# Two tiles' shared down products and the spread of the gates made in the middle of the expert loop

## What is computed

```
t, _ = token_mixer(h)                      # earlier stages
x  = x + gate1 * RMSNorm(t);  h = RMSNorm(x) * (1 + scale2) + shift2
eidx = top-8 of 64 experts per token;  w = gates (sum to 2.5)
routed = sum over the 8 of  w * ((silu(h @ w1[e]) * (h @ w3[e])) @ w2[e])
shared = (silu(h @ ws1) * (h @ ws3)) @ ws2
y = x + gate2 * RMSNorm(routed + shared)
```

## Time and profile before

| | |
|---|---|
| median of 3 runs | 1266.09 us (1265.21 to 1268.41) |
| the profiled execution, its time | 1263.9 us |
| its span, first to last instruction | 1262.2 us |
| PE busy | 1179.9 us, 93% of the span |
| DMA engines, 694 to 1167 us of the span | 90% or more busy, 396 to 414 GB/s |
| expert loop | from about 630 to 1219.5 us of the span |
| tail | from 1219.5 us to the end |

### The profile page before, as it was taken

The page is one execution under the profiler, slowest core; times in us unless marked ns, Lnnn a source line. Parts: engine busy times, 40 slices in busy tenths (PEclk is TensorE's granted clock), DMA queues, the critical chain, the costliest instruction groups (busy, mean ns, idle before and its releaser), DMA issues.

```text
span 1262.2 us, 25654 instructions
## 1 busy us (share of the span) xinstructions
PE 1179.9 (93%) x8947; PEld 849.8 (67%) x8948; DVE 556.5 (44%) x902; ACT 335.0 (27%) x631; POOL 524.5 (42%) x527
## 2 busy tenths in 40 slices
PE   5899999999999899968899999997799998999997
PEld 5599999999999899956655555553445554455442
DVE  0576676659568868136733322211122222222124
ACT  4522322322333442335211211111111111112112
POOL 1244444445448243410655444453345543444410
PEclk8899999999999999989999999998899999999999
DMA  9954245424421233309979999999999999999974
GB/s 300 307 167 151 85 149 165 148 85 150 150 83 34 67 100 100 117 1 382 356 291 393 396 396 409 409 409 414 412 408 409 407 403 401 402 404 404 371 289 168
DMA packets 160169, 337.35 MB, mean 267 GB/s; under 512 B 14686, under 2 KB 99242, under 8 KB 143728
## 3 DMA queue, kind: packets, MB, share of 16 engines
q1 hardware_dynamic: 140048, 295.55, 62.8%
q0 software_dynamic: 16656, 34.14, 7.2%
q10 hardware_dynamic: 3424, 7.09, 1.7%
HBM read 322.21 MB, written 33.30 MB: 282 GB/s over the span
## 4 chain that ended last, share of the span: by engine, by line
PE 71%; DMA 9%; SPq 7%; DVE 5%; issue 5%; POOL 2%; ACT 1%; DVEq 0%; ACTq 0%; POOLq 0%
PE ps L1697 22%; PE ps L1708 11%; PE ps L1459 10%; PE ps L1460 9%; PE ps L1461 9%; DMA w<-in_w_dram 6%; SPq L342 4%; DMA ring<-in_w_ada_dram 2%; SPq L347 2%; PE ps L1703 2%; PE ps L1775 1%; PE ps L1472 1%; PE ps L1414 1%; PE ps L1783 1%; SPq L302 1%
## 5 line engine op out<-in xcount | busy, mean ns | idle before, releaser
L1697 PE MATMUL ps<-w,xe 128*64 x3136 | 369.0, 389 | 35.0 <-DMA w<-in_w_dram 29.3
L1697 PEld LDWEIGHTS ps<-w,xe 128*64 128x64 f32 x3136 | 226.3, 140 | 174.6 <-issue 73.8
L510 POOL TENSOR_TENSOR wsplit<-ring,wsplit 128x1024 fp32r<-128x1024 f32 x80 | 194.6, 2433 | 286.5 <-ACT wsplit L711 276.8
L1459 PE MATMUL ps<-h_s_hi,wsplit 128*128 128x260 f32 x960 | 272.5, 284 | 0.0
L1461 PE MATMUL ps<-h_s_hi,wsplit 128*128 128x260 f32 x960 | 270.9, 282 | 0.0
L1460 PE MATMUL ps<-h_lo_m_hi,wsplit 128*128 128x260 f32 x832 | 235.0, 282 | 0.0
L1337 DVE TENSOR_TENSOR rs<-sg,ps 128x128 f32<-128x128 f32 x98 | 28.2, 288 | 378.7 <-ACT sg L959 378.7
L1708 PE MATMUL ps<-w,eactT 128*64 (+1 forms) x784 | 187.4, 599 | 0.0
L1459 PEld LDWEIGHTS ps<-h_s_hi,wsplit 128*128 128x128 f32 x960 | 180.8, 188 | 6.8 <-issue 5.9
L1461 PEld LDWEIGHTS ps<-h_s_hi,wsplit 128*128 128x128 f32 x960 | 180.9, 188 | 0.0
L711 ACT ACTIVATE wsplit<-ring 128x1024 fp32r<-128x1024 f32 x80 | 84.7, 1060 | 297.9 <-PE ps L1461 287.6
(11 more groups left out here) (323 smaller groups left out, 1346.0 us busy)
## 6 DMA issues: line engine op xcount, KB each, us to landing
w<-in_w_dram SPq DMA_DIRECT2D x192, 1024.0 KB, 19.7
ring<-in_w_in_dram SPq DMA_DIRECT2D x56, 512.0 KB, 4.0
ring<-in_w_ada_dram SPq DMA_DIRECT2D x12, 2048.0 KB, 9.0
act<-y_rows SPq DMA_DIRECT2D x4, 2048.0 KB, 14.2
ring<-y_rows SPq DMA_DIRECT2D x4, 2048.0 KB, 16.8
ring<-in_w_out_a_dram SPq DMA_DIRECT2D x8, 512.0 KB, 3.6
ring<-in_w_out_b_dram SPq DMA_DIRECT2D x8, 512.0 KB, 3.7
ring<-in_w_o_dram SPq DMA_DIRECT2D x8, 512.0 KB, 3.6
```

What stands on the lines that cost most here:

```text
L510: pool.tensor_tensor(wsplit[:, b, 1], raw[raw_slot], wsplit[:, b, 0], ALU.subtract).then_inc(S["w_lo"], 1)
L1459: mm(ps[:, bank + h, 0:HT], wsplit[:, b, 0, k, :], hi[:, k, p:q], start=(k == 0), stop=False)
L1697: ins = mm(ps[a * STRIP:(a + 1) * STRIP, 2 + f, 0:2 * P], xe[:, k, a * STRIP:(a + 1) * STRIP], w[a][:, k, :, f * P:(f + 1) * P], start=(k ...
```

## The change

SP reads ws2 as two DMAs of 512 KB in the middle of its refills, after that of expert 23, into rooms that are free by then (`ws2_in`), and no longer after the last expert's weights. PE's loop over the experts is cut in two after expert 29. Between the halves PE spreads the gates, into columns 384 to 511 of banks 2 and 3, and makes the shared down products of tiles 0 and 1, whose sums stay in banks 6, 7, 0 and 1 until the tail. For this the transposes of a pass move from banks 6 and 7 to columns 256 to 383 of banks 2 and 3, the banks of the up products. DVE makes gmat after its last pass, as before, but waits for PE's last transpose to be copied (ea_act), since it reads the same banks. gmat now lies in slot 5, and y_first of tile 0 and y_last of tile 3 come as two DMAs each, of three blocks and of one.

```diff
-        y_first = [blocks(t) for t in (xflat[:, 0:YF], slot_part(5, 0, YF), slot_part(0, 0, YF), slot_part(1, 0, YF))]
-        y_last = [blocks(t) for t in (slot_part(2, 0, YF), slot_part(3, 0, YF), slot_part(4, 0, YF), xflat[:, 0:YF])]
-        ws2_back = slot_part(5, YF, 2 * D).rearrange("p (k n) -> p k n", k=FT)
+        split = [(xflat[:, 0:3 * D], 3), (slot_part(5, YF + D, D), 1)]
+        y_first = [split] + [whole(t) for t in (slot_part(5, 0, YF), slot_part(0, 0, YF), slot_part(1, 0, YF))]
+        y_last = [whole(t) for t in (slot_part(2, 0, YF), slot_part(3, 0, YF), slot_part(4, 0, YF))] + [split]
+        ws2_in = [hflat[:, 0:D], xflat[:, 3 * D:4 * D]]
+        gmat = slot_part(5, YF, D).rearrange("p (b i h m) -> p b i h m", b=4, i=TT - 1, h=2)
...
-            with sp.Fori(1, E // DEEP) as g:
+            with sp.Fori(1, 4) as g:
+                for u in range(DEEP):
+                    refill(g * DEEP + u, g * DEEP + (u - DEEP), u)
+            sp.wait_ge(S["late_chain"], LA * TT)
+            for k in range(FT):
+                sp.dma_start(ws2_in[k], ws2[0, k * P:(k + 1) * P, :]).then_inc(w_late, 16)
+            with sp.Fori(4, E // DEEP) as g:
                 for u in range(DEEP):
                     refill(g * DEEP + u, g * DEEP + (u - DEEP), u)
...
-            sp.dma_start(ws2_back, w_src(ws2, 0, D)).then_inc(w_late, 16)
...
-                    act.activation(eactT[:, f, :], ps[:, 6 + f, 0:P], ACT.Copy).then_inc(S["ea_act"], 1)
+                    act.activation(eactT[:, f, :], ps[:, 2 + f, 2 * P:3 * P], ACT.Copy).then_inc(S["ea_act"], 1)
...
+            passes = dve.value_load(few[0:1, 2:3], min_val=E // 2, max_val=STEPS)
             dve.wait_ge(S["gp_pe"], 1)
-            link(tt(gpart, ps[:, 3, 0:P].rearrange("p (n k) -> p n k", k=4), m4[:, :].unsqueeze(1).to_broadcast([P, P // 4, 4]), ALU.mult))
+            dve.wait_ge(S["ea_act"], passes * 2)
+            link(tt(gpart, ps[:, 2, 3 * P:4 * P].rearrange("p (n k) -> p n k", k=4), m4[:, :].unsqueeze(1).to_broadcast([P, P // 4, 4]), ALU.mult))
...
-            with pe.Fori(0, E // DEEP) as g:
+            with pe.Fori(0, 5) as g:
+                for u in range(DEEP):
+                    expert(g * DEEP + u, u, g)
+            pe.wait_ge(S["last_pass_dve"], 2)
+            pe.wait_ge(S["late_chain"], LA * TT)
+            for b in range(4):
+                mm(ps[:, 2, 3 * P + 32 * b:3 * P + 32 * b + 32], spread[:, b * P:(b + 1) * P],
+                   gates[:, 0:TT - 1, :].rearrange("p i k -> p (i k)"), start=True, stop=True)
...
+            mark(ins, "gp_pe")
+            pe.wait_ge(w_late, 16 * C + 64)
+            shared_down(0)
+            shared_down(1)
+            with pe.Fori(5, E // DEEP) as g:
...
+            pe.wait_ge(S["gm_dve"], 2)
+            shared_down(2)
+            pe.wait_ge(y_first_in, 16 * TT)
             mark(gated_rows(0, 1, y_first), "early_pe")
+            gated_rows(1, 1, y_first)
             pe.wait_ge(S["xe_dve"], passes * 2 + 2)
-            shared_down(1)
             last_sums(0)
-            gated_rows(1, 1, y_first)
             pe.wait_ge(S["ex_yd"], passes + 2)
-            for n in range(2, TT - 1):
-                shared_down(n)
-                last_sums(n - 1)
-                gated_rows(n, 1, y_first)
+            shared_down(3)
+            last_sums(1)
+            gated_rows(2, 1, y_first)
+            last_sums(2)
+            gated_rows(3, 1, y_first)
             pe.wait_ge(S["yacc"], 1)
             shared_down(TT - 1)
             last_sums(TT - 2)
```

More of the change, by code:

```diff
@@ L124, in build_program @@
         yb = hflat[:, 2 * D:4 * D].rearrange("p (b d) -> p b d", b=2)
-        gmat = hflat[:, 0:D].rearrange("p (b i h m) -> p b i h m", b=4, i=TT - 1, h=2)
         xflat = act5[:, 0:R]
@@ L150, in slot_part, with whole @@
             return act5[:, a:a + n]
-        def blocks(t):
-            return t.rearrange("p (b d) -> p b d", b=4)
         YF = 4 * D
-        y_first = [blocks(t) for t in (xflat[:, 0:YF], slot_part(5, 0, YF), slot_part(0, 0, YF), slot_part(1, 0, YF))]
-        y_last = [blocks(t) for t in (slot_part(2, 0, YF), slot_part(3, 0, YF), slot_part(4, 0, YF), xflat[:, 0:YF])]
-        ws2_back = slot_part(5, YF, 2 * D).rearrange("p (k n) -> p k n", k=FT)
+        def whole(t):
+            return [(t, 4)]
+        split = [(xflat[:, 0:3 * D], 3), (slot_part(5, YF + D, D), 1)]
[3 more added lines that the diff above has]
+        gmat = slot_part(5, YF, D).rearrange("p (b i h m) -> p b i h m", b=4, i=TT - 1, h=2)
         x1b = [slot_part(0, YF, D), slot_part(0, YF + D, D), slot_part(1, YF, D), slot_part(1, YF + D, D), slot_part(2, YF, D)]
@@ L395, in tile_rows @@
                 at = i * P * TOPK + h * P * TOPK // 2
-                sp.dma_start(dst[i], y_rows[at:at + P * TOPK // 2, :].rearrange("(b p) d -> p b d", p=P)).then_inc(landed, 16)
+                for part, n in dst[i]:
+                    sp.dma_start(part.rearrange("p (b d) -> p b d", b=n),
+                                 y_rows[at:at + n * P, :].rearrange("(b p) d -> p b d", p=P)).then_inc(landed, 16)
+                    at += n * P
             sp.wait_ge(spill, 16 * TT)
             slot_free(E - 6)
-            sp.dma_start(ws2_back, w_src(ws2, 0, D)).then_inc(w_late, 16)
             slot_free(E - 5)
@@ L403, in _ @@
             x1_back(1)
-            sp.wait_ge(S["late_chain"], LA * TT)
             sp.wait_ge(S["last_pass_dve"], 1)
@@ L1351, in _ @@
                 dve.sem_inc(S["passed"], 1)
+            passes = dve.value_load(few[0:1, 2:3], min_val=E // 2, max_val=STEPS)
             dve.wait_ge(S["gp_pe"], 1)
-            link(tt(gpart, ps[:, 3, 0:P].rearrange("p (n k) -> p n k", k=4), m4[:, :].unsqueeze(1).to_broadcast([P, P // 4, 4]), ALU.mult))
+            dve.wait_ge(S["ea_act"], passes * 2)
+            link(tt(gpart, ps[:, 2, 3 * P:4 * P].rearrange("p (n k) -> p n k", k=4), m4[:, :].unsqueeze(1).to_broadcast([P, P // 4, 4]), ALU.mult))
             link(dve.tensor_reduce(gcol, gpart, AX.X, ALU.add))
             link(tt(gmat.rearrange("p b i h m -> p (b i h) m"), bc(gcol, P // 4), bm[:, :].unsqueeze(1).to_broadcast([P, P // 4, P // 4]), ALU.mult), "gm_dve", wait=False)
-            link(tt(gpart_s, ps[0:NS * TOPK, 2, 0:4], m4[0:NS * TOPK, :], ALU.mult))
+            link(tt(gpart_s, ps[0:NS * TOPK, 3, 3 * P:3 * P + 4], m4[0:NS * TOPK, :], ALU.mult))
             link(dve.tensor_reduce(gcol_s, gpart_s, AX.X, ALU.add))
@@ L1701, in act_T @@
             def act_T(f):
-                return tr(ps[:, 6 + f, 0:P], eact[:, f * P:(f + 1) * P], ident[:, :])
+                return tr(ps[:, 2 + f, 2 * P:3 * P], eact[:, f * P:(f + 1) * P], ident[:, :])
             def down_product(w, k, h):
@@ L1759, in expert, with shared_down @@
                         down_product(down, 1, 1).then_inc(S["ex_y"], 1)
-            with pe.Fori(0, E // DEEP) as g:
+            def shared_down(n):
+                i, f = order[n], bank_of[n]
+                rows = P if i < TT - 1 else LAST
+                for h in range(2):
+                    for k in range(FT):
+                        mm(ps[0:rows, f + h, :], scr[:, 2 + k, i * P:i * P + rows], ws2_in[k][:, h * 512:(h + 1) * 512],
+                           start=(k == 0), stop=False)
+            with pe.Fori(0, 5) as g:
[6 more added lines that the diff above has]
+                   gates[:, 0:TT - 1, :].rearrange("p i k -> p (i k)"), start=True, stop=True)
+            for h in range(2):
+                ins = mm(ps[32 * h:32 * h + 32, 3, 3 * P:3 * P + 4], spread[0:NS, 0:4 * NS],
+                         gates[0:NS, TT - 1, 4 * h:4 * h + 4], start=True, stop=True)
+            mark(ins, "gp_pe")
[3 more added lines that the diff above has]
+            with pe.Fori(5, E // DEEP) as g:
                 for u in range(DEEP):
@@ L1767, in _ @@
             passes = pe.value_load(few[0:1, 2:3], min_val=E // 2, max_val=STEPS)
[L1769 to L1776, removed]
             def gated_rows(n, h, src):
@@ L1782, in gated_rows @@
                     for b in range(4):
-                        ins = mm(ps[32 * b:32 * b + 32, f + c, :], gmat[:, b, i, h, :], src[i][:, b, c * 512:(c + 1) * 512],
+                        part, n = src[i][0] if b < src[i][0][1] else src[i][1]
+                        at = b % n * D + c * 512
+                        ins = mm(ps[32 * b:32 * b + 32, f + c, :], gmat[:, b, i, h, :], part[:, at:at + 512],
                                  start=False, stop=(h == 0))
@@ L1787, in last_sums @@
             def last_sums(n):
-                pe.wait_ge(y_last_in[order[n]], 16)
+                pe.wait_ge(y_last_in[order[n]], 16 * len(y_last[order[n]]))
                 mark(gated_rows(n, 0, y_last), "stat_mm")
[L1791 to L1801, removed]
             pe.wait_ge(S["gm_dve"], 2)
-            pe.wait_ge(y_first_in, 16 * (TT - 1))
+            shared_down(2)
+            pe.wait_ge(y_first_in, 16 * TT)
```

(9 more changed lines are left out.)

## The result

The changed kernel takes 1260.36 us (median of 13 runs, 1259.1 to 1265.17), the kernel before 1266.89 us beside it (13 runs). The ratio is 0.995 with a 95% interval of 0.994 to 0.996: 6.5 us or 0.5% faster. The forecast was 1261.1 us, within 1257.0 to 1265.5. In two later comparisons the same code gave 0.9958 [0.9943, 0.9974] and 0.9933 [0.9919, 0.9947].

A forecast was written before the change was run, and what follows sets the result against it. Two bounds take turns in the loop, full DMA engines and PE; then PE's tail is all on the path. -8.43 + 2.56 + 0.9 = -4.97 us, so 1261.1 us against a median of 1266.09, range 1257.0 to 1265.5.

The forecast's parts named there:

- What leaves the tail: Tail after the last pass: the gates' spread (1.17 us) and two shared products (7.26 us) leave it, 8.43 us less.
- the wait for gm_dve: Start of the tail: PE newly waits for DVE's gmat, priced at 0.9 us, range 0.2 to 1.3 us.
- The middle work costs nothing: Between passes 20 and 21: 8.43 us of work covered by 10.63 us of PE's waits ahead of pass 24; cost nothing.
- a branch into other code: Where PE's expert loop is cut: entering other code was said to cost too little to matter.
- ws2's bytes: SP's refills near 801 us: 1.049 MB at 409 GB/s delay every later landing, passes 24 and 45 included, by 2.56 us.
- the bound of 3.1 us: Upper bound for ws2's read, if gathers and scatters kept their share of the time, leaving weights 342 GB/s.
- The lower bound of 0: Lower bound for ws2's read: no cost if the DMA engines had gaps that the 1.02 share hides.
- the second rival's main case: Tail: y_last of tile 3, with 1.8 us margin, lands late; the whole rival, gain 0 to 3.5 us, had chance 0.27.
- Banks: Expert passes: moving the transposes into banks 2 and 3 was said to add nothing to a pass.
- The slower rival: Transposes in the up products' banks hold up each of 49 passes; a loss from 0.58 us a pass; chance 0.05.
- Its own signs of being wrong: Wrong if pass 45 moves by 0 or over 4 us, PE waits for y_last_in3, or a pass has grown.
- its first rival: ws2's bytes cost nothing (gain 7.5 us, 1258.6 us), or pass 45 starts warm (1.6 us more gained); chance together 0.13.

The follow-up runs named there:

- behind expert 53: The changed kernel with the middle work put after expert 53 (between passes 39 and 40), not after expert 29: 1268.51 us, ratio 1.0012 to the kernel before.
- the products in the tail: The changed kernel with the two shared products back in the tail, ws2's early read and the gates' spread kept: 1265.72 us, ratio 1.0004 to the kernel before.
- one profile with no byte moved: The kernel before with only the transposes moved to banks 2 and 3: 1265.28 us, ratio 1.0001; its one profiled execution took 1267.48 us.
- the comparison side by side: Changed kernel as it is, without ws2's read, and with ws2 read before the first refill, on one chip: ratios 0.9933, 0.9928, 0.9931 to the kernel before.

## Why the prediction was right, and where it was off

**What leaves the tail**: -8.43 us by the sum, 8.49 to 8.50 us less in three profiles, together with the wait for gm_dve. Undone alone, it took the whole gain away (1.0004). The two products' 7.26 us are the gain. Shown.

**The middle work costs nothing.** Shown, with room to spare: done twice (15.1 us of work with the gates) it gave 0.9944 beside 0.9933 to 0.9958, and without ws2's bytes pass 45 starts 542.6 us after pass 0 with the work and without it. The forecast start of pass 24, 927.4, was off: 933.38 in the first profile. 2.9 us of that lie ahead of the loop (pass 0 at 633.42, before at 630.50), and p24 - p0 is 299.96, 297.88 and 298.34 us, against 294.34 before. The sentence that a branch into other code costs too little to matter did not hold: in the first passes through the new code PE paused for 0.6 us (3.0 in the kernel with the work twice), which was covered, and behind expert 53 for 1.4 and 2.6 us, which was not.

**ws2's bytes, 2.56 us.** That they cost something is shown by the times: 0.9925 without the read and 0.9952 with it, over all comparisons. The size stays open between 1.9 and 3.4 us. By the products in the tail it is 1.9 to 2.3 us; by the tail, 8.49 us shorter in a kernel that is 6.1 us faster over all comparisons (0.9952), it is 2.4 us; by the kernels without the read 3.4 us. By the profiles pass 45 starts 3.7 to 6.0 us later. Of this the last four passes win back about 1.6 us in two of the three, where pass 45 began without a slow stretch (its up products took 6.26 us and not 7.8), which leaves 2.6 to 4.4 us at pass 48. But one profile with no byte moved came 3.3 us late at pass 45. The term of 2.56 us is inside all that; the bound of 3.1 us, taken as the greatest, may be too low. The lower bound of 0 fits only the comparison side by side, where the ratios differ by 0.0005.

**The wait for gm_dve, 0.9 us**: mis-sized; it is 0.14 us, and 0.13 and 0.14 in two further profiles. The prediction set a register load, taken at 0.6 us with the signal's way and at most 1.10, behind DVE's last transpose. The load (L1361, 0.31 us) ran beside the transpose: it began at 1223.6, and L1364 began at 1224.56, before the transpose ended at 1224.63. The range given, 0.2 to 1.3, missed the value by a hair.

**y_last of tile 3**: the second rival's main case did not come. No row of the chain in the tail waits for it, in any of the profiles.

**Banks**: 1.0001 alone, pass length 11.16 us. The slower rival did not come. By the Trainium skill's page "PSUM — Partial Sum Buffer", section "PSUM bank collisions raise a hardware error", the hardware doesn't stall engines that meet in a bank but raises an error. The measured zero agrees with that, but no run here is known to have put two engines into one bank at once.

**Its own signs of being wrong.** PE did not wait for y_last_in3. Pass 45 moved against pass 0 by 5.95, 3.84 and 4.26 us in the three profiles, in two of them beyond the 4 us that the prediction named, so by its own sign the step on the bytes is not confirmed in size. Passes had grown too, but in one profile of three and not with the banks alone. PE's waits for weights, forecast at 23 us, are 18.9, 25.6 and 24.1 us.

**The sum.** With 0.14 for the wait, -8.43 + 2.56 + 0.14 = -5.7 us; measured -6.5 us (-7.6 to -5.1), and -5.3 and -8.5 in the repeats. The forecast gain of 4.97 us was 1.5 us too small; the wait, priced 0.76 us too high, is half of that, and the other half is within the noise. The forecast time, 1261.1 us, came to within 0.7 us of 1260.36 partly by luck: it was counted from a median of 1266.09, and that of before was 1266.89 beside the changed kernel. What leaves the tail, its cover in the loop and the zero for the banks were right as steps.

## What to carry to other kernels

Work can be hidden in a loop whose weights are late, if it stands ahead of enough waiting: between passes 20 and 21, 8.2 us cost nothing, and 15.1 us did neither. So add up the waits that are left behind a place before you use it; behind expert 53 they were 4.4 us. Look for a second cost where the work cuts a loop in two. In the first passes through the new code PE paused for 0.6 to 3 us at a time (that this is the loading of the code was not tested). Ahead of long waits that was free; behind expert 53 it made 8.2 us of work cost 7.6. A DMA queue that runs dry is no proof of loss either: look whether anything waits for what it carries. A read moved ahead of a saturated stream is not free; try it where the DMA share is still below 1, which gave 2.9 us over all comparisons, though not clearly in the one where the kernels ran side by side. A tail that only waits behind its own engine gives back every microsecond taken from it, so look there first.

## What was not expected of the hardware

PE's register load ahead of each pass took up to 1.1 us in one execution. The line in after's first profile, then in its second (duration in ns, least, median, greatest):

```profile
L1759 PEldq TENSOR_LOAD <-table x49: 295/317/1107, 641.7 to 1220.4; - x49
```

```profile
L1759 PEldq TENSOR_LOAD <-table x49: 295/300/323, 639.4 to 1217.8; - x49
```

In the first, 21 passes that no wait, work or slow start explains are 0.15 to 1.0 us longer than 11.16, with rows such as this one:

```profile
736.03 1.08 PE L1718 MATMUL ps<-w,eactT 128*64 x4 [0.79 <-issue]
```

The code is the same, so this belongs to the execution. What makes the load slow stays open.

Pass 45's 64 up products begin fast in some executions and slowly in others, 1.6 us apart. The windows of its start, in the profile of before and in that of after (the granted clock is the third figure from the end):

```profile
1173.00:1181.00 8.00, 7.92 (x57) 4.86 (x57) 1.10 (x2) 0.28 (x1) 2.15 (x3) 0.79 1.01 367
```

```profile
1182.00:1190.00 8.00, 8.00 (x69) 4.92 (x69) 1.56 (x3) 0.83 (x3) 2.56 (x4) 1.00 1.00 355
```

PE ran part of the first stretch at 1.2 GHz and all of the second at 2.4. It had idled 3.09 us ahead of the one and 2.27 ahead of the other. In further profiles idle times of 2.96 to 3.31 us went with a slow start (six of them), 1.88 and 1.85 us, but 3.11 and 3.59 too, with a fast one. So the length of the idle time alone doesn't decide it. The prediction gave this a small chance as part of its first rival; it came in two profiles of three, and what it is worth in the medians can't be told apart from ws2's price.
